# Attention steps every seven tiles of strip matmuls, and a head's sum evacuated at the front of DVE's step

## The reference

```python
proj = u @ w_in                       # q and gate, 2048 -> 2 * 2048
z = einsum('bqkgd,bskd->bkgqs', qb, k) / sqrt(HEAD_DIM) + bias
mask = kpos[None, :] < qpos[:, None]  # strictly causal
log_keep = where(mask, log_sigmoid(-z), 0.0)
suffix = cumsum(log_keep, reverse=True) - log_keep
attn = where(mask, exp(log_sigmoid(z) + suffix), 0.0)
o = einsum('bkgqs,bskd->bqkgd', attn, v)
return (o * silu(gate)) @ w_out
```

## Time and profile before

| | |
|---|---|
| median of 3 runs | 1904.79 us |
| profiled execution | 1905.77 us, its span 1904.0 us |
| PE busy | 1748.4 us (92%) |
| DVE busy | 1110.5 us (58%) |
| ACT busy | 805.7 us (42%) |
| chain that ended last | PE 75%, DVE 13%, ACT 5%, issue 5% |
| matmuls of units, L641 + L642 + L643 into `PS` | 11040 |
| granted TensorE clock, mean | 0.956 |

### The profile page before, as it was taken

How to read it: one execution, slowest core, us unless ns; L and a number is a source line. 1 busy time by engine, 2 the same in 40 slices (tenths; PEclk the granted TensorE clock), 3 DMA queues, 4 the chain that set the end, 5 groups by cost and what they waited for, 6 DMA issues and landing times.

```text
span 1904.0 us, 35455 instructions
## 1 busy us (share of the span) xinstructions
PE 1748.4 (92%) x13991; PEld 1682.1 (88%) x13991; DVE 1110.5 (58%) x1869; ACT 805.7 (42%) x1196; POOL 247.6 (13%) x181
## 2 busy tenths in 40 slices
PE   6999999999997999975889999999989999799994
PEld 5999999999997999974889899998988888699993
DVE  4676656556766222249577677676765656622227
ACT  5434444443345222223255555556555555522222
POOL 1000000000000001014232222222221111011110
PEclk9999999999998999995899999999999999899995
DMA  8332222233321233235222222222214777423325
GB/s 245 96 100 73 83 87 87 88 88 88 99 74 37 83 94 92 84 99 167 72 70 67 67 67 57 78 67 68 58 55 147 213 229 220 124 78 88 88 78 164
DMA packets 279213, 191.57 MB, mean 101 GB/s; under 512 B 7899, under 2 KB 250715, under 8 KB 279003
## 3 DMA queue, kind: packets, MB, share of 16 engines
q1 hardware_dynamic: 276872, 183.16, 32.7%
q0 software_dynamic: 2176, 6.69, 1.0%
q10 hardware_dynamic: 68, 0.41, 0.1%
HBM read 174.26 MB, written 15.97 MB: 100 GB/s over the span
## 4 chain that ended last, share of the span: by engine, by line
PE 75%; DVE 13%; ACT 5%; issue 5%; DMA 1%; SPq 0%; POOL 0%; ACTq 0%; DVEq 0%; POOLq 0%
PE PS L641 22%; PE PS L643 21%; PE PS L642 21%; PE Z L887 2%; PE Z L641 1%; PE Z L643 1%; PE Z L642 1%; DVE Y L1673 1%; DVE WS L1427 1%; PE Z L897 1%; DMA xin<-in_x_prompt_dram 1%; DVE T L1699 1%; DVE T L1731 1%; ACT T L1211 1%; ACT T L1210 1%
## 5 line engine op out<-in xcount | busy, mean ns | idle before, releaser
L641 PE MATMUL PS<-U,WS 128*128 128x272 f32 x3680 | 1084.2, 295 | 61.6 <-DVE U L1680 34.2
L643 PE MATMUL PS<-U,WS 128*128 128x272 f32 x3680 | 1074.8, 292 | 0.0
L642 PE MATMUL PS<-U,WS 128*128 128x272 f32 x3680 | 1070.4, 291 | 0.0
L641 PEld LDWEIGHTS PS<-U,WS 128*128 128x128 f32 x3680 | 704.2, 191 | 72.6 <-issue 42.5
L642 PEld LDWEIGHTS PS<-U,WS 128*128 128x128 f32 x3680 | 704.4, 191 | 0.8
L643 PEld LDWEIGHTS PS<-U,WS 128*128 128x128 f32 x3680 | 703.8, 191 | 0.0
L1427 DVE TENSOR_TENSOR WS<-raw,WS 128x1024 fp32r<-128x1024 f32 (+1 forms) x234 | 285.5, 1220 | 428.1 <-ACT WS L1043 425.4
L1043 ACT ACTIVATE WS<-raw 128x1024 fp32r<-128x1024 f32 (+1 forms) x236 | 242.5, 1027 | 543.4 <-PE PS L643 536.8
L568 POOL TENSOR_TENSOR raw<-raw,GN 128x1024 f32<-128x1024 f32 x80 | 156.7, 1959 | 553.2 <-DMA raw<-in_b_w_in_dram 471.9
L580 POOL TENSOR_TENSOR T<-T 128x544 f32<-128x544 f32 x45 | 63.6, 1413 | 376.9 <-ACT T L1175 376.9
L577 POOL COPY T<-T 128x544 f32<-128x544 f32 x3 | 2.4, 793 | 636.0 <-ACT T L1175 577.6
(11 more groups left out here) (257 smaller groups left out, 2044.8 us busy)
## 6 DMA issues: line engine op xcount, KB each, us to landing
raw<-in_a_w_in_dram SPq DMA_DIRECT2D x80, 512.0 KB, 3.8
raw<-in_b_w_in_dram SPq DMA_DIRECT2D x64, 512.0 KB, 4.1
raw<-in_a_w_out_dram SPq DMA_DIRECT2D x32, 512.0 KB, 3.9
KPG<-in_cache_k_dram SPq DMA_DIRECT2D x64, 256.0 KB, 3.0
VPG<-in_cache_v_dram SPq DMA_DIRECT2D x64, 256.0 KB, 2.8
raw<-in_b_w_out_dram SPq DMA_DIRECT2D x32, 512.0 KB, 3.9
T<-scratch_x SPq DMA_DIRECT2D x32, 272.0 KB, 2.9
scratch_x<-T POOLq DMA_DIRECT2D x16, 272.0 KB, 3.6
```

The lines of the kernel that those rows point to most:

```text
L641: pe.matmul(psum, w_hi, x_hi, start=first, stop=False)
L642: pe.matmul(psum, w_hi, x_lo, start=False, stop=False)
L643: return pe.matmul(psum, w_lo, x_hi, start=False, stop=last)
```

## The change

The table of units is gone. Step a (0 to 63 over all rounds) begins at tile 56 + 7a of stage D, counted from the stage's first tile. `qk` of a head's first step stands ahead of tile 57 + 7a, `step_before` ahead of tile 60 + 7a, and `step_after` ahead of tile 65 + 7a, which is often in the next unit. Which unit's program on ACT and DVE holds a step stays as it was (the same 0, 1, 2, 3, 4, 4, 5, ...). Two things move there: the split of q1 (`q_split` and `q_rest` of g = 1) goes ahead of the unit's step, and `head_out` goes from the end of DVE's step to behind `exponent`. The last `pv` moves from tile 3 to tile 6 of unit 63.

```diff
-STEP_UNITS = (0, 1, 2, 3, 4, 4, 5, 6, 7, 8, 9, 10, 11, 11, 12, 13)
-STEPS_AT = {}
+STEP_TILES = 7
+STEPS_AT, LOGITS_AT, REST_AT, LATER_AT = {}, {}, {}, {}
 for a_ in range(4 * NH):
-    STEPS_AT.setdefault(FIRST_STEP + 2 * HEAD_STRIPS * (a_ // 16) + STEP_UNITS[a_ % 16], []).append((a_ // 16, a_ // 4 % GRP, a_ % 4))
+    tile_ = UT * FIRST_STEP + STEP_TILES * a_
+    step_ = (a_ // 16, a_ // 4 % GRP, a_ % 4)
+    STEPS_AT.setdefault((tile_ + 4) // UT, []).append(step_)
+    LOGITS_AT[divmod(tile_ + 1, UT)] = step_
+    REST_AT[divmod(tile_ + 4, UT)] = step_
+    LATER_AT[divmod(tile_ + 9, UT)] = step_
...
-                steps_ = STEPS_AT.get(n, ())
-                for t, (k, g, s) in enumerate(steps_):
-                    if s == 0 and c == 0:
-                        qk(k, g, 0)
-                    if c == ((2,) if len(steps_) == 1 else (1, 5))[t]:
-                        step_before(k, g, s)
-                    if c == (UT if t == len(steps_) - 1 else 4):
-                        step_after(k, g, s)
+                at = (n, c)
+                if at in LOGITS_AT and LOGITS_AT[at][2] == 0:
+                    qk(*LOGITS_AT[at])
+                if at in REST_AT:
+                    step_before(*REST_AT[at])
+                if at in LATER_AT:
+                    step_after(*LATER_AT[at])
...
-                if n == TAIL and c == 3:
+                if n == TAIL and c == 6:
                     pv(NKV - 1, GRP - 1, 3)
...
+                if kind == "q" and g == 1:
+                    q_split(n // 2 - 1, k, g)
                 for step_ in STEPS_AT.get(n, ()):
                     step(*step_)
-                if kind == "q":
+                if kind == "q" and g != 1:
                     q_split(n // 2 - 1, k, g)
...
                 if before:
                     exponent(*before)
+                if s == 1 and (k or g):
+                    head_out(*((k, g - 1) if g else (k - 1, GRP - 1)))
                 if s == 0:
                     scaled(k, g, 0)
...
                 if s < 3:
                     scaled(k, g, s + 1)
-                if s == 1 and (k or g):
-                    head_out(*((k, g - 1) if g else (k - 1, GRP - 1)))
...
+                if kind == "q" and g == 1:
+                    q_rest(k, g)
                 for t, step_ in enumerate(STEPS_AT.get(n, ())):
                     step(*step_, next_unit if t == 0 else None)
-                if kind == "q":
+                if kind == "q" and g != 1:
                     q_rest(k, g)
```

More of the change, by code:

```diff
@@ L873, in attention @@
                         turn_kv(TURN_AT[n], 0)
-                    if c == (UT if steps_ else 6):
+                    if c == (UT if n in STEPS_AT else 6):
                         turn_kv(TURN_AT[n], 1)
-                if n == TAIL and c == 3:
+                if n == TAIL and c == 6:
                     pv(NKV - 1, GRP - 1, 3)
```

## The result

The changed kernel takes 1935.3 us (median, 1933.8 to 1940.6) against 1904.8 (1903.0 to 1906.4) for the kernel before, timed in turn on one chip. The ratio is 1.0165 with a 95% interval of 1.0144 to 1.0186: slower by 30 us. The forecast was 1915.6 with a range up to 1925. The direction was right; the time lies 20 us above the forecast and 10 above the range.

A forecast was written before the change was run, and what follows sets the result against it. PE was taken to wait on the order of each step's chain through DVE and ACT. Middle rounds +5.3, first +1.5, last +1.0, clock +1.7, tail +1.3 made +10.8 us: 1915.6 against the median, range 1894 to 1925.

The forecast's parts named there:

- Terms (a) to (g): PE's idle time in a middle round, from q1 in unit 3 to the turn: 10.2 us, where it was 7.4 and 7.7.
- q1: Term (a), unit 3: rest of step 2 waits for exponent behind strip and q_rest; 3.2 us, bounds 2.3 and 3.9.
- step 4: Term (b), unit 4: ACT's high for unit 5 precedes step 3's exponential; PE waits 0.9 us, bounds 0 and 1.5.
- q2 and q3: Term (c), units 6 and 8: q_rest ahead of exponent is no longer done in time; 0.7 us each, 1.4 together.
- the gate: Term (d), unit 1: exponential starts 4.35 us behind high because tables change twice for the sigmoid; PE waits 0.6 us.
- unit 11: Term (f): exponent of step 11 waits for the v strip, so at_rest ends late for pv; 1.2 us.
- the turn: Term (g), units 13 and 14: PE reaches the turns earlier and waits for the turned tiles; 2.4 us together.
- The last round: Gates replace k, v and q strips; the 4.0 us wait in unit 11 stays, idle time goes from 12.2 to 13.2.
- The tail: Last pv stands three tiles later with page loads behind it, new scores start earlier; +1.3 us, bounds -2 and +4.
- Clock: Waits above 3 us bring one more slow-clock stretch at 1.7 us each; +1.7 us, bounds -3.4 and +7.
- Rival 1: Seven tiles are enough, the step's chain has slack nearly everywhere: 1884 us, 1897 with half the terms; chance 0.22.
- Rival 3: GpSimd's fold meets a DVE copy ahead of exponent or q_rest, up to 1.9 us each: 1925 us; chance 0.13.

## Why the prediction was right in direction and short by 20 us

**Terms (a) to (g), the middle round: right.** The waits of round 1, as the excess of PE's start over its usual pace, are 3.4 for q1 (predicted 3.2), 0.8 for step 4 (0.9), 0.7 and 0.9 for q2 and q3 (0.7 each), 0.6 for the gate (0.6), 1.2 for unit 11 (1.2), 0.7, 1.6 and 0.5 around the turn (2.4). Idle time of the two middle rounds is 9.1 and 10.3, predicted 10.2 each: +4.2 together where +5.3 was predicted. In length they grew by 5.9, but unevenly, by 1.2 and 4.7: q2 and q3 cost 1.2 and 1.5 in round 2, and the kernel before has a stretch of slow clock in round 1, the changed one in round 2. The first round grew by 1.5 (+1.5). Most signs to look for came: `exponent` 20.2, a little above the 13 to 19, with q1's waits at 2.3, 3.4, 3.4 and 3.3 us, so three over 3 and not four; `head_out` nothing; turned tiles 6.6, 5.1 of them for ACT's copies. Two came less well: `at_rest` has 15.8, counted with the waits marked `issue`, and not about the 11.2 of before; and the middle rounds took 121.8 and 124.4, not 123 to 124. So six differences of two long chains, which I trusted least, were the good part.

**The last round, +1.0 predicted, +10.1 measured: the step that failed.** I wrote that gates stand in the place of k, v and q strips there, and gave them no term of their own: "the wait of 4.0 in its unit 11 stays, 12.2 becomes 13.2". PE's idle time of that round became 21.4. Three places make most of it. At the head of unit 63 PE waits 5.5 us, where it waited 1.5. At the end of unit 9, behind another gate, waits of 1.1 and 2.0 end at 1413.0 and 1415.6 us, where there was one of 1.3. The wait in unit 11 became 5.7; 4.0 of it stayed as I had it, and the other 1.7 goes without the fold. I had worked the chain through one middle round and carried it over, though the earlier trace rows show that a gate puts 4.35 us between `high` and the exponential, and ACT's busy time in the earlier trace rows (75.1 against 68.1) tells that there are more of them. The time from the start of one `later` to the end of the next `sp_rest` is read from the traces: in round 1 it is 4.7 to 6.6 us in before (7.5 at the turn) and 4.6 to 9.5 in after; in the last round the gate steps of units 9 and 11 take 9.0 and 8.8 in before, 10.3 and 12.3 in after, and without the fold 7.3 and 8.8 in before, 8.5 and 10.8 in after. The place has less slack and the chain of unit 11 is longer besides, since strip and `high` of a border now fall inside it.

**The tail, +1.3 predicted, +7.9 and +1.2 measured.** I counted three tiles for the last `pv`, and not that the last `later` lands at tile 2 of unit 63, with `new_logits` behind it. Putting it back gives 7.1 us. Of the last round's and the tail's excess of 19.2 us over before, this is shown; the gates give 4.0 more by the difference of the two pairs of medians, which is not clear of the intervals. Together that is 11 us; they were tested apart, so that they add is not shown. Of the rest, (a) is 3.4 as in every round. The clock is next.

**Clock, +1.7 predicted, about +4.9 measured.** Stretches at the lower level of 1.2 GHz go with the long waits of the end. Here are the three of 6.8 us (granted clock the third number from the end):

```profile
1432.40:1439.20 6.80, 3.27 (x12) 2.98 (x13) 5.33 (x9) 2.52 (x6) 1.91 (x1) 0.50 0.01 2
1459.70:1466.50 6.80, 4.61 (x81) 4.61 (x82) 2.04 (x4) 1.55 (x2) 0.83 (x1) 0.50 0.26 81
1470.00:1476.80 6.80, 5.42 (x35) 4.43 (x36) 2.98 (x13) 0.84 (x4) 0.00 (x0) 0.50 0.01 2
```

Each begins while PE still waits: the first at 1432.4, 2.2 us into the wait that ends at 1435.9, so that PE works for only 3.3 of its 6.8 us. A matmul starts there every 0.23 us in place of 0.126. At half pace a stretch costs half of the time that PE works in it, and not half of its length. Over units 7 to 64 that is an estimate of 14.4 us in after and 9.5 in before: +4.9, of which 3.8 from unit 49 on, most of the 4.6 by which PE's busy time grew there. It comes on top of the waits and follows them: the runs that took such waits away took their stretch with them in part. That the clock by itself would do something at equal waits was not tried.

**Rivals.** Rival 1 fell with the waits for `exponent`: its point of decision was (b) to (g) under 3 us a round, and by the list above they are 7.0. The half that it was right in is `head_out`, worth 6 us at once. Rival 3 named the time nearest to the result and is wrong in its mechanism, as the two kernels without the fold show. The exclusion that the earlier trace rows show is there in after too, as the rule of the Trainium skill has it (SBUF — State Buffer, section Who interferes with whom): with a fold beside them `at_rest` (L1742) and the mask's product (L1721) take 2.28 and 2.15 us in place of 0.55 and 0.42, and end 0.3 to 0.4 us behind its end. Here of DVE and then of POOL:

```profile
1458.66 2.28 DVE L1742 TENSOR_TENSOR U<-T,U 128x384 fp32r<-128x384 f32 x1
```
```profile
1458.62 1.91 POOL L573 TENSOR_TENSOR raw<-raw,GN 128x1024 f32<-128x1024 f32 x1 [5.26 <-DMA raw<-in_b_w_in_dram]
```

**What stays open.** 2.5 us of the 28.4 stand ahead of the first step. A slow stretch of 3.4 us at 60 us appears there in after and in most other profiles, but not in that of before; other kernels with the fold reach unit 7 at 950.2 to 952.3, so most of it is variation. And of the last round's 19.2 about 8 us are (a), clock and the waits at the end of unit 9 in shares that no run separates. The fold is not among them in sum.

## What to carry to other kernels

A chain of steps is to be laid out by the length of each step's chain, not evenly. Here the fixed work of a unit (`high`, strip, `low`, 3.1 us on two engines) belongs to eight tiles, so that the steps that share a unit have short chains and can stand four tiles apart, and the others need their eight. Four tiles were not free: with `head_out` in front PE still waits 2.7 us for `at_rest` there in round 1. Moving every step to seven takes slack from twelve steps to save those, and cost 36.6.

When one period of a loop is worked out and carried to the others, list first what the last one does differently (here three more gates, and nothing behind it to cover the end): that is where a tightened schedule breaks first. And a wait of 5 us that the profile names may be only what fills another wait: take away both before calling either a cause.

## What was unexpected of the hardware

The fold on GpSimd is worth 24 to 26 us over 80 folds, 0.3 us a fold on average, though only some of them meet a DVE instruction on the path. The waits of the kernel before for `head_out` fell from 16.5 to 9.0 us without the fold. The lower clock can come while TensorE still waits and pass within the wait in part, so the length of a slow stretch is not its price: of 37.6 us at 1.2 GHz in units 7 to 64 of after, TensorE worked in 28.7. And equal waits do not bring equal stretches: the q1 waits of rounds 1, 2 and 3 are 3.2 us each in the profile of after, and only that of round 2 has a slow stretch with it (1231.0 to 1234.4 us). Round 1 has a granted clock of 1.00, and so has round 3 as far as 1405 us.
